# Chunked attention with its division deferred to the output stage, and with transposes ahead of the values matmuls

## The chip, the cores and the metric

The kernel runs on one core of a Trainium2 chip. The core has a matrix engine (TensorE, PE in the profile), VectorE (DVE), ScalarE (ACT), GpSimd (POOL) and SyncE (SP), which here does nothing but issue DMAs. Each engine works through its own instructions in program order; semaphores tie the engines together. The metric is the time of one execution on the device in microseconds, the median of several runs.

## What is computed

One layer of a streaming encoder: a combined input projection, two groups of attention heads, one output projection, a gated per-layer embedding and a LayerNorm. SEQ is 4096, D_MODEL 1024, all in float32. The change is in group A and in what reads its result.

```
def chunk_relbias_attention(q, k, v, rel_bias):      # 8 heads of 64, chunks of 64
    ...
    scores = jnp.einsum('bnqhd,bnkhd->bnhqk', qc, kb) * (d ** -0.5)   # own chunk and 8 before
    scores = scores + bias[None, None]
    scores = jnp.where(valid[None, :, None, None, :], scores, -jnp.inf)
    probs = jax.nn.softmax(scores, axis=-1)
    out = jnp.einsum('bnhqk,bnkhd->bnqhd', probs, vb)
...
ya = ya * jax.nn.silu(ag)
mix = jnp.concatenate([ya, yb], axis=-1) @ w_out     # yb: the sliding-window group
h = alpha * x + mix
h = h + jax.nn.sigmoid(h @ w_ple_gate) * (p @ w_ple_proj)
x = layer_norm(h, ln_g, ln_b)
```

## The kernel before

Every float32 factor of a product is split in a high and a low part of type fp32r (ScalarE copies the high part, VectorE subtracts it), so that two or three matmuls stand for one exact product. The program has four stages, written one behind the other for each engine.

**Projections** write q, k, v and the gates to DRAM.

**Stage A**, chunked attention. A unit is one head and one tile of 128 tokens (t, 0 to 31), 256 units in all; a turn of the hardware loop is two heads, 64 units. A tile attends to n = min(5, t + 1) tiles of 128 keys. Each engine has a function `a_step(it, i)` that says what it does in step i, each part with a lag: `a_unit(it, i, 4)` is the unit that was new four steps ago. For one unit: `a_scores` on TensorE writes scores into PSUM banks 0 and 1 (the only pair, `psum[:, 0:2]`); VectorE adds the bias and takes the maximum (L1115), then scales the maximum (L1130); ScalarE takes the exponential and its sum (L807); VectorE inverts the sum (L1125); ScalarE (L833), or for three tiles of eight VectorE (L1137), multiplies the probabilities by it; TensorE transposes them in five 128x128 pieces (`a_transpose`, L1404, lag 4) into banks 2 and 3 or 4 and 5; ScalarE and VectorE split them into pt_hi (L825) and pt_lo (L1103). For two units together `a_values` (lag 7) multiplies with v into bank 6 or 7. Its 128 output rows are two halves, by v's high and low part: ScalarE copies the lower 64 rows (L816), VectorE adds them to the upper ones (L1151). GpSimd multiplies four tiles' result with the gate (L683), and SyncE stores it to y_d and loads the next gate.

In a step TensorE issues first `a_values`, then `a_transpose`, then `a_scores` of the unit after the current.

**Stage B**, sliding-window attention: 64 units of four chunks; GpSimd applies the gate (L690), SyncE stores to y_d. At its end the weights of stage C are loaded and split in strips.

**Stage C**, the output, one tile of 128 tokens at a time. TensorE's loop: `mix(t + 1)`, 48 matmuls of 512 columns; `ple(t)`, 12; `gate(t)`, 48; `transpose_h(t + 1)`, eight transposes (L1542), which wait for the residual. VectorE's `c_step(t)`: y_lo of tile t + 2 (L1241), p_lo, the residual h of tile t + 1 (L1255), hT_lo, the LayerNorm of tile t (to L1297). ScalarE: y_hi of t + 2 (L898), p_hi, the sigmoid, hT_hi. GpSimd: the LayerNorm's scale and shift (L696, L698). SyncE, in this order:

```
def stage_c(t, i, more=True):
    sp.wait_ge(p_split, t + 1)
    load_tile(t + 2, i % 2)          # y_raw <- y_d, p_raw <- pT
    sp.wait_ge(h_done, t + 1)
    load_x(t + 1)                    # x_nat
    store_out(t, i % 3)              # waits for shifted, GpSimd's last pass on tile t
```

Since `store_out(t - 1)` stands ahead of `load_tile(t + 2)`, a tile of y is asked for only when the output of a tile three behind it is finished.

## Time and profile before

| | us |
|---|---|
| median of 3 runs | 2842.0 (2839.82 to 2842.2) |
| profiled execution, its span | 2843.8 |
| projections, to about | 1166 |
| stage A | 1166 to 1735 |
| stage B | 1735 to about 1990 |
| from B to C | about 1990 to 2022 |
| stage C | 2022 to 2843 |
| TensorE busy | 2692.4 (95%) |
| VectorE busy | 1398.1 (49%) |
| ScalarE busy | 1192.5 (42%) |
| GpSimd busy | 336.2 (12%) |

The shares are means over stages that differ much, so the stages are read one by one. TensorE's busy time is from modelled ends of pipelined matmuls that overlap; what a row of matmuls costs is read from the start of one to the start of the next. A name such as L1115 is a line of the kernel above. "Releaser" is what ended an engine's idle time.

### The profile page before, as it was taken

How to read it: one execution, taken by the hardware profiler on the slowest of the kernel's cores; microseconds unless marked ns; L12 is line 12 of the kernel's file. 1: busy time of each engine (PE TensorE's matmuls, PEld its weight loads, DVE VectorE, ACT ScalarE, POOL GpSimd, SP SyncE). 2: the span in 40 equal slices, each digit the busy share in tenths (PEclk: the TensorE clock that was granted, in tenths of full speed). 3: DMA queues.
4: the chain of work that ended last, by engine and by line, in shares of the span. 5: the costliest groups of instructions: out<-in, count | busy, mean ns of one | idle time of the engine just before them, and what ended most of it. 6: DMA issues, size and time to landing. Idle time of an engine off the chain costs nothing.

```text
span 2843.8 us, 40981 instructions
## 1 busy us (share of the span) xinstructions
PE 2692.4 (95%) x14544; PEld 2325.9 (82%) x14544; DVE 1398.1 (49%) x3367; ACT 1192.5 (42%) x2448; POOL 336.2 (12%) x227
## 2 busy tenths in 40 slices
PE   7999999999999999889989898987799999999997
PEld 5888888988888889878888888887688888888886
DVE  5211156232111461589989996778433334333343
ACT  3111122231111221589989997778322222222222
POOL 2000000000000000011111111334112221122211
PEclk9999999999999999999999997778899999999999
DMA  6431246453312463887767647785422211222111
GB/s 196 161 120 63 77 100 148 151 193 126 122 63 77 99 146 111 202 188 160 163 146 161 154 101 163 184 196 145 128 73 72 72 59 61 72 72 72 57 62 54
DMA packets 279246, 339.32 MB, mean 119 GB/s; under 512 B 81712, under 2 KB 201536, under 8 KB 274880
## 3 DMA queue, kind: packets, MB, share of 16 engines
q1 hardware_dynamic: 277648, 335.67, 43.8%
q0 software_dynamic: 1456, 1.86, 0.2%
q8 instruction: 76, 1.25, 0.2%
q14 instruction: 66, 0.54, 0.1%
HBM read 211.10 MB, written 127.41 MB: 119 GB/s over the span
## 4 chain that ended last, share of the span: by engine, by line
PE 71%; DVE 9%; issue 8%; ACT 6%; DMA 5%; POOL 1%; SPq 0%; ACTq 0%; DVEq 0%; POOLq 0%
PE psum L1338 68%; DVE pt_lo L1103 3%; ACT pt_hi L825 2%; ACT prob L807 2%; DMA y_d<-y_b 1%; DMA av<-v_d 1%; DMA x_raw<-in_xT 1%; PE psum L1542 1%; DVE y_a L1151 1%; ACT y_low L816 1%; DVE prob L1137 1%; PE psum L1489 1%; ACT prob L833 1%; POOL y_b L690 1%; ACT prob_b L855 0%
## 5 line engine op out<-in xcount | busy, mean ns | idle before, releaser
L1338 PE MATMUL psum<-x_hi,w_hi 128*128 128x512 f32 x1408 | 549.5, 390 | 20.1 <-DVE x_lo L1008 18.2
L1338 PE MATMUL psum<-x_hi,w_lo 128*128 128x512 f32 x1408 | 549.2, 390 | 0.0
L1338 PE MATMUL psum<-x_lo,w_hi 128*128 128x512 f32 x1408 | 549.1, 390 | 0.0
L1338 PEld LDWEIGHTS psum<-x_hi,w_hi 128*128 128x128 f32 x1408 | 265.3, 188 | 75.6 <-issue 18.2
L1338 PEld LDWEIGHTS psum<-x_lo,w_hi 128*128 128x128 f32 x1408 | 265.2, 188 | 55.3
L1338 PEld LDWEIGHTS psum<-x_hi,w_lo 128*128 128x128 f32 x1408 | 265.1, 188 | 55.1
L683 POOL TENSOR_TENSOR y_a<-y_a,g_a 64x512 f32<-64x512 f32 x64 | 81.4, 1272 | 1582.6 <-DVE y_a L1151 1582.6
L1338 PE MATMUL psum<-wo_hi,y_hi 128*128 128x512 f32 x512 | 204.8, 400 | 15.5 <-DVE y_lo L1241 10.0
L1404 PE MATMUL psum<-ident,prob 128*128 128x128 f32 x1200 | 182.4, 282 | 38.8 <-DVE pt_lo L1103 33.1
L1115 DVE CUSTOM_DVE_ANT_0 prob<-psum,bias 128x640 f32<-128x640 f32 (+4 forms) x256 | 198.8, 777 | 32.5 <-issue 30.3
L807 ACT ACTIVATE prob<-prob,small 128x640 f32<-128x640 f32 (+4 forms) x256 | 202.2, 790 | 27.2 <-DVE small L1130 22.4
L1241 DVE TENSOR_TENSOR y_lo<-y_raw,y_hi 128x1024 fp32r<-128x1024 f32 x32 | 39.2, 1225 | 347.4 <-ACT y_hi L898 347.4
L1103 DVE TENSOR_TENSOR pt_lo<-psum,pt_hi 128x640 fp32r<-128x640 f32 (+4 forms) x256 | 197.2, 770 | 15.3 <-ACT pt_hi L825 10.2
L1338 PE MATMUL psum<-wo_hi,y_lo 128*128 128x512 f32 x512 | 201.4, 393 | 0.0
L1338 PE MATMUL psum<-wo_lo,y_hi 128*128 128x512 f32 x512 | 201.0, 393 | 0.0
L1338 PE MATMUL psum<-wg_hi,hT_lo 128*128 128x512 f32 x512 | 199.4, 390 | 0.0
L1338 PE MATMUL psum<-wg_hi,hT_hi 128*128 128x512 f32 x512 | 199.2, 389 | 0.0
L1338 PE MATMUL psum<-wg_lo,hT_hi 128*128 128x512 f32 x512 | 199.2, 389 | 0.0
L1404 PEld LDWEIGHTS psum<-ident,prob 128*128 128x128 f32 x1200 | 129.9, 143 | 62.5 <-issue 55.0
L1048 DVE TENSOR_TENSOR stage_out<-psum,work 128x512 f32<-128x512 f32 x64 | 44.3, 692 | 273.2 <-ACT work L767 273.2
L1022 DVE TENSOR_TENSOR stage_out<-psum,stage_out 128x512 fp32r<-128x512 f32 x72 | 49.8, 691 | 251.6 <-ACT stage_out L742 226.6
L1338 PE MATMUL psum<-pt_hi,av 128*128 128x256 f32 x720 | 172.2, 275 | 0.8 <-DVE pt_lo L1103 0.8
(165 smaller groups left out, 5597.0 us busy)
## 6 DMA issues: line engine op xcount, KB each, us to landing
qk_d<-stage_out SPq DMA_DIRECT2D x80, 512.0 KB, 2.8
w_raw<-in_w_in SPq DMA_DIRECT2D x24, 1024.0 KB, 5.6
x_raw<-in_xT SPq DMA_DIRECT2D x32, 512.0 KB, 4.6
g_d<-stage_out SPq DMA_DIRECT2D x64, 256.0 KB, 2.0
bq_d<-stage_out SPq DMA_DIRECT2D x64, 256.0 KB, 4.1
v_d<-stage_out SPq DMA_DIRECT2D x32, 512.0 KB, 2.9
bq<-bq_d SPq DMA_DIRECT2D x64, 256.0 KB, 4.4
y_raw<-y_d SPq DMA_DIRECT2D x32, 512.0 KB, 4.8
```

The costliest lines, as they stand in the source:

```text
L683: pool.tensor_tensor(y_a[:, s, :], y_a[:, s, :], g_a[:, s, :], ALU.mult).then_inc(y_gated, 1)
L690: pool.tensor_tensor(yb, yb, g_b[:, s, :, :].rearrange("p h t -> p (h t)"), ALU.mult).then_inc(by_gated, 1)
L807: act.activation(prob[:, r, NBW - n * P:NBW], prob[:, r, NBW - n * P:NBW], ACT.Exp, bias=a_col(A_SHIFT, r), scale=SCALE, accum_out=a_col(A ...
L816: act.activation(y_low[:, pr % 2, :], psum[HEAD:P, 6 + pr % 2, 0:2 * P], ACT.Copy).then_inc(y_low_ready, 1)
L825: act.activation(pt_hi[:, (t // 2) % 2, e + BAND - n:e + BAND, e * P:e * P + P], src.rearrange("p (j q) -> p j q", q=P), ACT.Copy).then_in ...
L1022: dve.tensor_tensor(stage_out[:, slot, 1, :].bitcast(f32r), psum[:, bank, :], stage_out[:, slot, 0, :], ALU.subtract).then_inc(acc_free, 1)
L1048: dve.tensor_tensor(stage_out[:, r % 2, 0, :], psum[:, r % 8, :], work[:, r % 2, :], ALU.mult).then_inc(acc_free, 1)
L1103: dve.tensor_tensor(pt_lo[at], src.rearrange("p (j q) -> p j q", q=P), pt_hi[at].bitcast(f32), ALU.subtract).then_inc(probsT_split, 1)
L1115: dve.tensor_tensor_reduce(out=prob[:, r, NBW - n * P:NBW].rearrange("p (a b) -> p a b", a=2), in0=psum[:, 0:2, 0:n * P // 2], in1=bias[:, ...
L1241: dve.tensor_tensor(y_lo[:, :, :], y_raw[:, s, :, :], y_hi[:, :, :].bitcast(f32), ALU.subtract).then_inc(y_split, 1)
L1338: return pe.matmul(dst, lhs, rhs, start=start, stop=stop)
L1404: last = pe.transpose(psum[:, b, (j % 4) * P:(j % 4) * P + P], prob[:, t % RING, NBW - (n - j) * P:NBW - (n - j - 1) * P], ident[:, :])
```

## The change

The softmax's division is taken out of stage A. Scores and bias are combined so that their minimum serves directly as the exponential's bias, and the sums stay in `a_sum`; VectorE inverts the 32 sums of a head at once. The unnormalized result, still in its two halves, is copied by ScalarE (128x512, four tiles at once) and stored to `ya_d`. After the last head the inverses are transposed by TensorE, copied by ScalarE and stored to `ra_d`; stage B's first scores on TensorE wait for that copy. Sum of the halves, division and gate are now in stage C, on GpSimd, in `y_tile`. The split of the values matmuls into two parts and the order on TensorE are new, and the lags are shorter. The residual works in place in h (three slots), into which x is loaded.

```diff
 # SyncE, stage C
             def load_tile(t, s):
-                sp.dma_start(y_raw[:, s, :, :], y_d[:, bass.ds(t * P, P)].rearrange("(k p) t -> p k t", p=P)
+                cols = bass.ds(t * P, P)
+                sp.dma_start(y_two[:, s, :, :], ya_d[:, :, :, :, cols].rearrange("k c h d t -> (h d) (k c) t")
+                             ).then_inc(y_two_loaded[s], 16)
+                sp.dma_start(g_c[:, s, :, :], g_d[0:D_A, cols].rearrange("(k p) t -> p k t", p=P)
+                             ).then_inc(g_loaded[s], 16)
+                sp.wait_ge(g_scaled, t)
+                for hd in range(2):
+                    sp.dma_start(r_c[hd * HEAD:hd * HEAD + HEAD, :, :],
+                                 ra_d[:, hd, cols].unsqueeze(0).to_broadcast([HEAD, KT // 2, P])).then_inc(r_loaded, 16)
+                sp.dma_start(y_raw[:, s, KT // 2:KT, :], yb_d[:, cols].rearrange("(k p) t -> p k t", p=P)
                              ).then_inc(y_loaded[s], 16)
...
-            def stage_c(t, i, more=True):
-
+            def stage_c(t, i, stored, more=True):
+
+                slot = (i + 1) % 3
+                if stored is not None:
+                    sp.wait_ge(out_stored[slot], stored + 16)
+                load_x(t + 1, slot)
                 if more:
                     sp.wait_ge(p_split, t + 1)
                     load_tile(t + 2, i % 2)
-                sp.wait_ge(h_done, t + 1)
-                load_x(t + 1)
                 store_out(t, i % 3)
...
 # GpSimd
+            def y_tile(t, s, first=False):
+
+                two = y_two[:, s, :, :].rearrange("p (k c) t -> p k c t", c=2)
+                pool.wait_ge(y_two_loaded[s], 8 * (t - s) + 16)
+                if not first:
+                    pool.wait_ge(y_split, t - 1)
+                pool.tensor_tensor(y_raw[:, s, 0:KT // 2, :], two[:, :, 0, :], two[:, :, 1, :], ALU.add).then_inc(y_joined, 1)
+                pool.wait_ge(g_loaded[s], 8 * (t - s) + 16)
+                pool.wait_ge(r_loaded, 32 * t + 32)
+                pool.tensor_tensor(g_c[:, s, :, :], g_c[:, s, :, :], r_c[:, :, :], ALU.mult).then_inc(g_scaled, 1)
+                pool.wait_ge(y_joined, t + 1)
+                pool.wait_ge(g_scaled, t + 1)
+                pool.tensor_tensor(y_raw[:, s, 0:KT // 2, :], y_raw[:, s, 0:KT // 2, :], g_c[:, s, :, :], ALU.mult
+                                   ).then_inc(y_ready, 1)
...
+            with pool.Fori(0, 5) as it:
+                for i in range(6):
+                    y_tile(6 * it + i + 2, i % 2)
+                    scale_shift(6 * it + i, i % 3)
...
 # ScalarE
             def a_step(it, i):
-                unit = a_unit(it, i, 1)
+                unit = a_unit(it, i, 7)
+                if unit and unit[2] % 4 == 3:
...
+                    act.activation(y_a[:, slot, :], psum[:, 6 + quad % 2, :], ACT.Copy).then_inc(y_copied, 1)
+                unit = a_unit(it, i, 0)
...
             def y_tile_hi(t, s, first=False):
                 act.wait_ge(y_loaded[s], 8 * (t - s) + 16)
+                act.wait_ge(y_ready, t + 1)
...
 # TensorE
-            def a_values(u, pair, s, pr):
-                pe.wait_ge(probsT_split, u + 3)
-                pe.wait_ge(y_summed, pair + 1)
+            def a_values(u, it, quad, s, pr, part):
+
                 first_tile = 2 * pr - (BAND - 1)
...
+                order = [i for i in (1, 2, 0, 3, 4, 5) if first_tile + i >= 0]
+                half = (len(order) + 1) // 2
...
             def a_step(it, i):
-                unit = a_unit(it, i, 7)
-                if unit and unit[2] % 2 == 1:
-                    u, s, t = unit
-                    a_values(u, (A_TURN // 2) * it + (i - 7) // 2, s, t // 2)
-                unit = a_unit(it, i, 4)
+                unit = a_unit(it, i, 2)
                 if unit:
                     u, s, t = unit
-                    by_vector = t % 8 in VECTOR_NORMS
-                    a_transpose(u, t, normed[by_vector], norms(A_TURN - 1, by_vector) * it + norms(i - 4, by_vector))
-
+                    a_transpose(u, t)
+                for part, lag in ((1, 6), (0, 5)):
+                    unit = a_unit(it, i, lag)
+                    if unit and unit[2] % 2 == 1:
+                        u, s, t = unit
+                        a_values(u, it, (i - lag) // 4, s, t // 2, part)
```

On TensorE in the middle of stage A, before: a step with values, then one without, each instruction with its waits; `ident,prob` are transposes, `pt,av` values, `ak,aq` scores.

```order
L1338 MATMUL psum<-pt_hi,av 128x256 [waits y_summed,probsT_split]
L1338 MATMUL psum<-pt_lo,av 128x256
L1338 MATMUL psum<-pt_hi,av 128x256
L1338 MATMUL psum<-pt_lo,av 128x256
L1338 MATMUL psum<-pt_hi,av 128x256
L1338 MATMUL psum<-pt_lo,av 128x256
L1338 MATMUL psum<-pt_hi,av 128x128
L1338 MATMUL psum<-pt_lo,av 128x128
L1404 MATMUL psum<-ident,prob 128x128 [waits probsT_split,normed0]
L1404 MATMUL psum<-ident,prob 128x128 x4
L1338 MATMUL psum<-ak,aq_hi 128x320 [waits scores_used]
L1338 MATMUL psum<-ak,aq_hi 128x320
```

The same place after: in each step the transposes, then one half of a pair's values, then the scores.

```order
L1388 MATMUL psum<-ident,prob 128x128 [waits probsT_split,exp_done]
L1388 MATMUL psum<-ident,prob 128x128 x4
L1322 MATMUL psum<-pt_hi,av 128x256
L1322 MATMUL psum<-pt_lo,av 128x256
L1322 MATMUL psum<-pt_hi,av 128x256
L1322 MATMUL psum<-pt_lo,av 128x256
L1322 MATMUL psum<-pt_hi,av 128x128
L1322 MATMUL psum<-pt_lo,av 128x128
L1322 MATMUL psum<-ak,aq_hi 128x320 [waits scores_used]
L1322 MATMUL psum<-ak,aq_hi 128x320
L1322 MATMUL psum<-ak,aq_lo 128x320 x2
```

All values of a pair (eight rows here, twelve for a full band) stood in one step ahead of the transposes; now six stand in every step, behind them.

On SyncE in the loop of stage C, before; `out<-h` is the store of a tile, which waits for GpSimd's last pass.

```order
L614 DMA out<-h 128x1024 [waits shifted]
L559 ISA [waits p_split]
L559 DMA y_raw<-y_d 128x8x128
L561 DMA p_raw<-in_pT 128x2x128
L565 ISA [waits h_done]
L565 DMA x_nat<-in_x 128x1024
L614 DMA out<-h 128x1024 [waits shifted]
```

On SyncE in the same loop, after:

```order
L613 DMA out<-h 128x1024 [waits shifted]
L562 ISA [waits out_stored2]
L562 DMA h<-in_x 128x1024
L544 ISA [waits p_split]
L544 DMA y_two<-ya_d 128x8x128
L546 DMA g_c<-g_d 128x4x128
L550 DMA r_c<-ra_d 64x4x128 [waits g_scaled]
L550 ISA
L550 DMA r_c<-ra_d 64x4x128
L552 DMA y_raw<-yb_d 128x4x128
L558 DMA p_raw<-in_pT 128x2x128
L613 DMA out<-h 128x1024 [waits shifted]
```

x has moved ahead of the tile, and the tile's one DMA of y has become five; the store that waits for `shifted` is still ahead of all of them.

On GpSimd in the loop of stage C, before:

```order
L696 TENSOR_TENSOR h<-h,lng 128x1024 [waits normalized]
L698 TENSOR_TENSOR h<-h,lnb 128x1024 [waits scaled]
L695 REGISTER_ALU
L696 TENSOR_TENSOR h<-h,lng 128x1024 [waits normalized]
L698 TENSOR_TENSOR h<-h,lnb 128x1024 [waits scaled]
```

On GpSimd in the same loop, after:

```order
L702 TENSOR_TENSOR h<-h,lng 128x1024 [waits normalized]
L704 TENSOR_TENSOR h<-h,lnb 128x1024 [waits scaled]
L691 TENSOR_TENSOR y_raw<-y_two 128x512 [waits y_split,y_two_loaded1]
L693 ISA [waits g_loaded1]
L694 TENSOR_TENSOR g_c<-g_c,r_c 128x512 [waits r_loaded]
L695 REGISTER_ALU
L697 TENSOR_TENSOR y_raw<-y_raw,g_c 128x512 [waits g_scaled,y_joined]
L702 TENSOR_TENSOR h<-h,lng 128x1024 [waits normalized]
L704 TENSOR_TENSOR h<-h,lnb 128x1024 [waits scaled]
```

Each tile has three passes over 128x512 in front of the two over 128x1024 that it had.

## Rows read from the trace of the kernel before

**Rows 1.** The windows view, by stage: busy us per engine, granted clock, DMA share, GB/s.

```profile
66.00:1166.00 1100.00, 1100.00 (x5569) 942.41 (x5570) 328.95 (x529) 216.10 (x365) 1.25 (x2) 1.00 0.40 120
1166.00:1735.00 569.00, 504.04 (x3666) 452.13 (x3664) 509.49 (x1764) 523.65 (x1058) 81.43 (x64) 0.97 0.70 157
...
2022.00:2843.00 821.00, 804.96 (x3656) 667.65 (x3656) 303.15 (x542) 210.11 (x234) 148.18 (x62) 0.99 0.21 66
```

**Rows 2.** Groups by line, 1280 to 1720 us: busy us, mean ns | idle before.

```profile
L833 ACT ACTIVATE prob<-prob,small 128x640 f32<-128x640 f32 (+2 forms) x128 | 101.3, 791 | 0.0
...
L1151 DVE TENSOR_TENSOR y_a<-psum,y_low 64x256 f32<-64x256 f32 x103 | 42.2, 410 | 0.9
L1137 DVE TENSOR_SCALAR prob<-prob,small 128x640 f32<-128x640 f32 (+1 forms) x77 | 40.3, 524 | 0.0
L816 ACT ACTIVATE y_low<-psum 64x256 f32<-64x256 f32 x103 | 39.3, 381 | 4.0 <-PE psum L1338 1.5
```

**Rows 3.** The chain of what ended last, in stage A: start, us, what.

```profile
1490.36 0.71 DVE pt_lo L1103
...
1507.55 0.71 DVE pt_lo L1103
...
1515.95 2.04 PE psum L1338 x16
```

**Rows 4.** The timeline in stage A, TensorE and VectorE: start, us, instruction.

```profile
1505.07 0.73 PE L1404 MATMUL psum<-ident,prob 128*128 128x128 f32 x5
...
1505.55 0.54 PE L1338 MATMUL psum<-ak,aq_hi 128*128 128x320 f32 x2
...
1506.28 0.74 PE L1404 MATMUL psum<-ident,prob 128*128 128x128 f32 x5
...
1507.31 0.56 PE L1338 MATMUL psum<-ak,aq_hi 128*128 128x320 f32 x2 [0.30 <-DVE small L1115]
...
1508.30 0.82 DVE L1115 CUSTOM_DVE_ANT_0 prob<-psum,bias 128x640 f32<-128x640 f32 x1
```

**Rows 5.** The chain over the whole span, end of the first head.

```profile
1205.35 33.59 DMA av<-v_d
```

**Rows 6.** The timeline of VectorE: first tile of head 1, last tile of head 7.

```profile
1240.22 0.29 DVE L1115 CUSTOM_DVE_ANT_0 prob<-psum,bias 128x128 f32<-128x128 f32 x1
...
1720.08 0.82 DVE L1115 CUSTOM_DVE_ANT_0 prob<-psum,bias 128x640 f32<-128x640 f32 x1
```

**Rows 7.** The chain in stage C: two groups of transposes of h.

```profile
2480.62 0.87 PE psum L1542 x8
...
2506.02 0.87 PE psum L1542 x8
```

**Rows 8.** The timeline in stage C, GpSimd, SyncE, ScalarE and VectorE.

```profile
2492.60 2.39 POOL L698 TENSOR_TENSOR h<-h,lnb 128x1024 f32<-128x1024 f32 x1
2495.01 0.37 SPq L614 DMA_DIRECT2D out<-h  x1
2495.92 0.38 SPq L559 DMA_DIRECT2D y_raw<-y_d  x1
2500.34 1.06 ACT L898 ACTIVATE y_hi<-y_raw 128x1024 fp32r<-128x1024 f32 x1 [6.56 <-DMA y_raw<-y_d]
2502.91 1.22 DVE L1255 SCALAR_TENSOR_TENSOR h<-x_nat,psum 128x1024 f32<-128x1024 f32 x1
```

**Rows 9.** Costliest groups on the page: GpSimd's gating in stage A.

```profile
L683 POOL TENSOR_TENSOR y_a<-y_a,g_a 64x512 f32<-64x512 f32 x64 | 81.4, 1272 | 1582.6 <-DVE y_a L1151 1582.6
```

**Rows 10.** The timeline from B to C, TensorE and GpSimd [idle before <-releaser].

```profile
1977.70 1.08 PE L1489 MATMUL psum<-ident,prob_b 128*128 128x128 f32 x4 [3.41 <-DVE ptb_lo L1174]
...
1999.83 0.79 PE L1338 MATMUL psum<-wo_hi,y_hi 128*128 128x512 f32 x1 [10.04 <-DVE y_lo L1241]
...
2002.28 2.03 POOL L690 TENSOR_TENSOR y_b<-y_b,g_b 64x512 f32<-64x512 f32 x1 [3.76 <-DMA g_b<-g_d]
...
2021.79 0.79 PE L1338 MATMUL psum<-wo_hi,y_hi 128*128 128x512 f32 x1 [5.49 <-DVE wp_lo L1228]
```

More of the change, by code:

```diff
@@ L78 @@
 ALPHA32 = float(np.float32(ALPHA))
-def norms(v, by_vector):
-    n = (v + 1) // 8 * len(VECTOR_NORMS) + sum(t < (v + 1) % 8 for t in VECTOR_NORMS)
-    return n if by_vector else v + 1 - n
 def b_unit(u):
@@ L201, in build @@
         lng, lnb = (sb(n, [P, D_MODEL]) for n in ("lng", "lnb"))
-        h = sb("h", [P, 3, D_MODEL])
+        h1, h2 = (sb(n, [P, D_MODEL]) for n in ("h1", "h2"))
+        sb("strip_end", [P, D_MODEL])
+        h0 = sb("h0", [P, D_MODEL])
+        g_c = sb("g_c", [P, 2, KT // 2, P])
+        r_c = sb("r_c", [P, KT // 2, P])
+        y_hi, y_lo = (sb(n, [P, KT, P], f32r) for n in ("y_hi", "y_lo"))
+        h = (h0, h1, h2)
         stage.close()
@@ L522, in _ @@
             sp.sem_inc(p_over, 1)
-            for q in range(QSLOTS):
-                load_gate(0, q)
             for part in range(JB, PARTS):
@@ L622, in _ @@
             sp.sem_inc(b_over, 1)
+            for t in range(2):
+                load_p(t, t)
             sp.wait_ge(cw_split, len(strips))
@@ L928, in _ @@
             p_tile_hi(1, 1, True)
+            act.wait_ge(cw_split, len(strips))
             hT_tile_hi(0)
```

266 lines of the change are left out of this document (125 added, 141 removed).

## The prediction

> **What bounds the kernel now.** I first cut the span by stage [rows 1]. The projections (66 to 1166 us) keep TensorE busy for every microsecond and are not touched. Chunked attention (stage A, 1166 to 1735) has TensorE busy 504 of 569 us, VectorE 509 and ScalarE 524: three engines near their limit. Sliding-window attention (stage B, 1735 to 1990) does the same work before and after. The output stage (stage C, from 2022) is TensorE again, 805 of 821 us. A reader should see two kinds of stage: in A a cut on VectorE and ScalarE can pay, in C only something that makes TensorE wait can change the time.
>
> **Stage A, what goes.** Between 1280 and 1720 us [rows 2] ScalarE spends 101.3 us in the normalizing copy L833 and 39.3 in the 64-row copy L816, and VectorE 40.3 in L1137 and 42.2 in the add L1151. All four go, with two one-column operations per tile on VectorE. ScalarE gets one 128x512 copy per four tiles; at the price of the 128x640 passes (about 0.8 us) that is 0.2 us a tile. Both engines fall from about 90% (524 and 509 of 569 us) to some 65 to 75%, so neither sets the pace.
>
> **Stage A, what is late next.** TensorE has the same matmuls as before. Its cost for two tiles comes from start to start [rows 3, 4]: one score group with twelve values matmuls 2.04 us, the other score group 0.73 (1505.55 to 1506.28), two groups of transposes 0.48 each (1505.07 to 1505.55). The sum is 3.73, or 1.87 us a tile. A second ring is as long: scores write a single pair of banks, so they start at 1507.31, the VectorE pass on them at 1508.30, and it ends at 1509.12, after which the next scores may start: 1.81 us. The new order fits both: in the 0.9 us in which VectorE holds the banks, TensorE has the transposes (0.48) and half of a pair's values ((2.04 - 0.73) / 2 = 0.66). So TensorE is the bound, at 1.87 or above. What stands behind it is the wait of the transposes for pt_lo, which follows the bias pass on VectorE and now ends at about the time the scores end; I add 0.1 and take 1.97. The period now is 17.19 us for eight tiles, 2.15 each (in [rows 3] 1490.36 and 1507.55 are the same step of the pattern of eight).
>
> Seven heads run from 1240.22 to 1720.08 [rows 6]. Each has 28 full tiles, which gain 28 x 0.18 = 5.0 us, and four short ones, for which I take 1 us together: 7 x 6 = 42 us. The first head ends in a wait for the load of av, issued at 1205.35 and landed 33.59 us later behind everything else in the queue [rows 5]. Faster compute doesn't shorten that; four gate loads of 128 KB fewer do, by about 2 us. **Stage A: -44 us.** Bounds: -60 if TensorE runs at 1.87 with no wait and the short tiles gain 2 us a head, -20 if the waits between the three engines bring the period to 2.08. The reciprocals are turned into rows once, by two transposes and one copy, in front of B: 1 to 2 us, taken as covered by the shorter drain (lag 6 for 7). B itself does the same work.
>
> **Stage C, the wait that the change adds.** Here the division and the sum of the halves now lie. Follow one tile [rows 7, 8]. The transposes of h start at 2480.62, and the next ones at 2506.02: 25.4 us, all of it TensorE. Beside it runs a chain which nearly fills that time. GpSimd's second pass on the output ends at 2494.99 (2492.60 + 2.39), SyncE stores it at 2495.01 and only then, in program order, issues y_raw for two tiles on, at 2495.92. It lands and ScalarE splits it from 2500.34. VectorE subtracts, and after that, again in program order, does the residual, 2502.91 to 2504.13. The transposes need that residual, and it is there 1.9 us before they are due. So TensorE bounds this stage with less than 2 us to spare.
>
> The change puts three things into that chain. First, SyncE now issues x in front of the tile, then y_two, g_c, twice r_c, y_raw and p. By the end of r_c the queue has moved, beyond what it moves now by the end of y_raw, x (0.5 MB) and g_c and r_c (0.25 MB each): 1.05 MB with y_two in y_raw's place. The rate of the full queue follows from stage C: 66 GB/s at a share of 0.21 [rows 1] make 0.31 MB per us. That is 3.3 us: r_c lands at about 2503.7, and y_two at about 2502.3. Second, GpSimd does three passes of 512 columns, for which the row is its pass over 64x512, 1.27 us [rows 9]. The join runs under the r_c load; the scaling of the gate and the product follow it: 2503.7 + 2.6 = 2506.3. Third, ScalarE and VectorE go on as before, y_hi to the end of the residual 3.8 us (2500.34 to 2504.13): 2510.1. The transposes are due at 2506.02 and start at 2510.1. **+4.1 us a tile**, and since the next tile's chain starts with these transposes, the delay is not absorbed but comes again with each.
>
> Bounds. Below: y_two lands no earlier than y_raw does now, plus 0.5 us for the x issue ahead of it (2500.8), and GpSimd's three passes are in order, 3.8 us: 2504.6, residual 2508.4, so +2.4. Above: seven DMAs' own overhead and slow small packets, another 2 us: +6.1.
>
> The array's clock comes on top. After an idle stretch of 3.41 us in stage B [rows 10] it stands at the lower of its two levels: four transposes take 1.08 us there, where stage C's eight take 0.87 [rows 7]. Transposes after each stall would take twice as long, 0.87 us more, and they are on the chain; the matmuls after them are not, since TensorE then has time to spare. I take +0.8, nearly every tile.
>
> The Trainium skill ("TensorE: Matmul & The Clock Gate", in "Why this matters for your kernels") says that idle gaps between bursts of matmuls send the array back to its lower clock; by its rule the 0.87 comes in all tiles, 2 us more in the total than I take. [rows 10] agree. On the load the skill ("DMA: Bandwidth & Descriptors", in "Anatomy of one DMA") has a variable part of bytes by 436 GB/s; as an estimate by it the 1.05 MB would take 2.4 us for my 3.3, and the total would be some 27 us lower. Stage C's row shows 0.31 MB per us, and the measurement decides.
>
> The loop loads tiles 2 to 31; tile 2's load waits for no store, and the last h isn't behind a tile's load. That leaves 29 groups of transposes: 29 x (4.1 + 0.8) = **+142 us**. Bounds 29 x 2.4 = 70 and 29 x 6.9 = 200.
>
> **From B to C.** The first tile's load now needs GpSimd, which is in order behind B's last gating, 2002.28 + 2.03 = 2004.3 [rows 10]. Three passes, y_hi and y_lo (about 2.2) put the first product at 2010.3, where it starts at 1999.83 now. Three more DMAs sit ahead of B's last gate loads, some 2 us. It ends in the same way: the array waits until 2021.79 for the last strips, whose splits stand behind y_hi of tile 1 and so behind that product. **+12 us**, bounds +5 (the strips, not the product, are late) and +18.
>
> **The sum** against the profiled execution: 2843.8 - 44 + 142 + 12 = 2953.8 us. The median of the runs is 1.8 below the profiled span: 2952 us, 3.9% slower.
>
> **Rivals.**
> 1. *Stage C absorbs it; the result is faster.* If y_hi could start by about 2502.2, 1.9 us later than now, TensorE would never wait, and the whole would be 2842 - 44 + 9, about 2807. For it: engines other than TensorE are idle most of stage C (GpSimd 148 of 821 us by [rows 1]), and the y load was always waited for, not computed. Against it: even the bound from below puts y_hi at 2504.6, 2.4 us past that point, and two GpSimd passes (2.5 us) alone exceed the slack. It needs GpSimd's passes at less than half of their row and x's transfer hidden. 8%.
> 2. *Stage C stalls by the lower bound with no clock loss, and A gains all:* 2842 - 60 + 70 + 5 = 2857, still 0.5% slower: one end of the main case, within its chance.
> 3. *Stage A gains nothing.* The new order might trade the saturated engines for the ring of scores and bias pass: at 2.08 us a tile or more, A gives 20 or less, and the sum is 2976 or more, about 2980. For it: that ring measures 1.81 us before any jitter, and TensorE 1.87. Against it: the two overlap fully on paper. 12%.
> 4. *The change does not do what it says in A:* if the first half of the values waits for pt_lo of its own pair, the order brings nothing over values first. Its pair is three steps behind the scores on VectorE and five on TensorE, so it doesn't wait. Only the division's cut would count; 2970. 3%.
>
> **How the numbers follow.** Main case, 75%: 2952, with its own range of 2857 to 3010. Rival 3 and 4, 15%: 2970 to 2980. Rival 1, 8%: 2807. Between them, C stalling by 1 to 2 us only, 2%: about 2840. The range is 2865 to 3010: the main case and rivals 3 and 4, short of the corner in which all of the main case's bounds fall low together. A run of this kernel repeats within 0.1% and a comparison can tell about 0.2%. Faster by over 0.2%: 0.09; within: 0.02; slower: 0.89.
>
> **What the changed profile would show.** In stage A bias passes 1.9 to 2.0 us apart, ScalarE and VectorE near 70%, heads of some 61 to 64 us, and waits of the transposes on pt_lo. In stage C transposes of h 29.5 to 30.5 us apart, each after an idle stretch of 3 to 4 us that VectorE's residual ends, ScalarE's y_hi released by GpSimd, and a granted clock visibly under 1. I am wrong if the transposes of h stay 25.4 us apart, or if y_hi starts less than 2 us later in its tile than now.

## The result, and the profile after

The changed kernel takes **3048.6 us** (median of 4 runs, 3045.5 to 3054.7) against 2842.1 (2839.8 to 2845.4): a ratio of 1.0724, 95% interval 1.0708 to 1.0740. It is 7.2% slower. The forecast was 2952, 3.9% slower, with a range up to 3010: the sign was right, the size was not.

The windows view of the changed kernel, by stage (columns: window, its length, busy us of PE, PEld, DVE, ACT, POOL with instruction counts, granted TensorE clock, DMA share, GB/s):

```profile
66.00:1166.00 1100.00, 1098.20 (x5573) 940.94 (x5571) 329.28 (x536) 217.31 (x369) 0.00 (x0) 1.00 0.40 120
1164.00:1675.00 511.00, 484.86 (x3695) 454.84 (x3696) 385.79 (x1050) 401.39 (x858) 0.00 (x0) 0.97 0.76 177
1676.00:1956.00 280.00, 214.52 (x1372) 207.12 (x1370) 196.43 (x448) 197.80 (x719) 94.19 (x67) 0.73 0.71 173
1976.00:3052.00 1076.00, 879.28 (x3656) 721.85 (x3656) 303.50 (x543) 213.76 (x235) 263.16 (x152) 0.90 0.28 72
```

The last row answers to stage C's in [rows 1]: the same 3656 matmuls and transposes, in 1076 us for 821, at a clock of 0.90 for 0.99. TensorE was 98% busy there and is 82% busy now. The second row answers to stage A's: VectorE and ScalarE are at 75 and 79%, at or a little above the forecast's 65 to 75%, and the stage is shorter.

Five points of the program, read from the two timelines, cut the 209.0 us between the two profiled executions (2843.8 and 3052.8) into pieces:

| stretch | before | after | difference | forecast |
|---|---|---|---|---|
| start to first bias pass | 1167.4 | 1164.4 | -3.0 | 0 |
| first to last bias pass (A) | 552.6 | 490.3 | -62.4 | |
| last bias pass to B's first scores | 15.3 | 11.7 | -3.6 | A in all: -44 |
| B's first scores to C's first product | 264.5 | 289.7 | +25.2 | |
| C's first product to its loop | 22.0 | 20.0 | -2.0 | B to C: +12 |
| C's loop to the end | 822.0 | 1076.8 | +254.7 | +142 |

The first row isn't the change's doing: in the profiles of kernels below that are the same up to this point the first bias pass starts at 1163.6 to 1167.3.

**Stage C, one period.** The timeline of the changed kernel from a tile's last pass on GpSimd to the next transposes of h; it answers to [rows 7, 8]. Numbers in brackets are the idle time before an instruction and what ended it. The last line is from the kernel before, at the same point of its loop.

```profile
2491.85 2.39 POOL L704 TENSOR_TENSOR h<-h,lnb 128x1024 f32<-128x1024 f32 x1
...
2494.27 0.37 SPq L613 DMA_DIRECT2D out<-h  x1
2494.83 0.36 SPq L562 DMA_DIRECT2D h<-in_x  x1
2495.39 0.56 SPq L544 DMA_DIRECT2D y_two<-ya_d  x1
2496.04 0.87 SPq L546 DMA_DIRECT2D g_c<-g_d  x1
2497.01 1.44 SPq L550 DMA_DIRECT2D r_c<-ra_d  x2
...
2501.24 1.29 POOL L691 TENSOR_TENSOR y_raw<-y_two 128x512 f32<-128x512 f32 x1 [7.00 <-DMA y_two<-ya_d]
2506.08 1.28 POOL L694 TENSOR_TENSOR g_c<-g_c,r_c 128x512 f32<-128x512 f32 x1 [3.55 <-DMA r_c<-ra_d]
2507.51 1.26 POOL L697 TENSOR_TENSOR y_raw<-y_raw,g_c 128x512 f32<-128x512 f32 x1
...
2511.37 1.22 DVE L1239 SCALAR_TENSOR_TENSOR h<-h,psum 128x1024 f32<-128x1024 f32 x1
...
2512.64 1.97 PE L1538 MATMUL psum<-ident,h 128*128 128x128 f32 x8 [5.43 <-DVE h L1239]
...
2480.45 1.03 PE L1542 MATMUL psum<-ident,h 128*128 128x128 f32 x8
```

The chain runs as the prediction describes it: store, loads, join, scaling, product, split, residual, transposes; then through the LayerNorm to the next store at 2528.10. Two links are longer than forecast. GpSimd waits for r_c until 2506.08, 11.8 us behind the store, where I had 8.7. And all the transposes behind a stall run at the lower clock: 1.97 us, after an idle stretch of 5.43, for 1.03 to 1.04 in the same view of the kernel before. (The 0.87 of [rows 7] is from the chain, which counts only from the end of the matmul in front.) From store to store the loop takes 34.15 us on average over 28 tiles; before it took 25.41.

**Where r_c is late.** The DMA view of stage C (2020 to 3000 us), median us from issue to landing:

```profile
y_two<-ya_d SPq DMA_DIRECT2D x28, 512.0 KB, 5.6
r_c<-ra_d SPq DMA_DIRECT2D x58, 128.0 KB, 7.6
y_raw<-yb_d SPq DMA_DIRECT2D x29, 256.0 KB, 8.6
g_c<-g_d SPq DMA_DIRECT2D x28, 256.0 KB, 6.1
```

128 KB of r_c, issued 1.6 us behind 512 KB of y_two, land later after their issue than y_two after its own. Each of its two loads reads four rows of 128 reciprocals and writes them to 64 partitions: 256 packets of 512 bytes, all from the same four places.

What the DMA engines do meanwhile, the windows view shows for the period above (columns: window, its length, busy us of GpSimd, granted clock, DMA share, GB/s):

```profile
2495.00:2502.00 7.00, 0.76 (x1) 1.00 0.99 282
2502.00:2505.00 3.00, 0.54 (x1) 1.00 0.31 72
```

From 7.7 us behind the store the rate falls to a quarter, and the engines are busy a third of the time; r_c is there at 2506. In the mean of 26 tiles the rate from 7 to 10 us behind the store is 57 GB/s. The queue isn't full there; it moves slowly.

**From B to C.** GpSimd at the end of B:

```profile
1933.01 1.26 POOL L682 TENSOR_TENSOR y_b<-y_b,g_b 64x512 f32<-64x512 f32 x1 [1.85 <-DMA g_b<-g_d]
1945.35 1.26 POOL L682 TENSOR_TENSOR y_b<-y_b,g_b 64x512 f32<-64x512 f32 x1 [11.09 <-DMA g_b<-g_d]
1948.44 1.25 POOL L682 TENSOR_TENSOR y_b<-y_b,g_b 64x512 f32<-64x512 f32 x1 [1.82 <-DMA g_b<-g_d]
1949.65 1.25 POOL L691 TENSOR_TENSOR y_raw<-y_two 128x512 f32<-128x512 f32 x1
```

The last gate load but one lands 11 us late. On SyncE the five loads of tile 0 are issued just ahead of it (1931.91 to 1935.13), the slow r_c among them. And the join of tile 0 stands behind all 64 gate passes.

### The profile page after: what moved, and what is told of

It is laid out like the page before. It is cut to its first block, busy times and chain, and to the rows that moved or that the text cites. A ratio compares the mean times of both kernels' runs of the same rounds, so it can differ in the third digit from the quotient of the medians.

```text
span 3052.8 us, 39860 instructions
## 1 busy us (share of the span) xinstructions
PE 2738.8 (90%) x14546; PEld 2375.1 (78%) x14546; DVE 1269.0 (42%) x2638; ACT 1068.3 (35%) x2225; POOL 376.1 (12%) x257
## 4 chain that ended last, share of the span: by engine, by line
PE 44%; issue 16%; DVE 15%; DMA 10%; POOL 9%; SPq 3%; ACT 3%; DVEq 0%; POOLq 0%; ACTq 0%
PE psum L1322 41%; DMA y_two<-ya_d 5%; DVE pt_lo L1132 5%; POOL h L704 2%; POOL h L702 2%; DMA g_b<-g_d 2%; PE psum L1538 2%; POOL g_c L694 1%; POOL y_raw L697 1%; DVE sg L1254 1%; DVE h L1257 1%; DMA yb_d<-y_b 1%; DMA av<-v_d 1%; DVE h L1239 1%; ACT y_hi L907 1%
## 5 line engine op out<-in xcount | busy, mean ns | idle before, releaser
L682 POOL TENSOR_TENSOR y_b<-y_b,g_b 64x512 f32<-64x512 f32 x64 | 90.5, 1415 | 1794.6 <-DVE y_b L1197 1655.2
L1322 PE MATMUL psum<-wo_hi,y_hi 128*128 128x512 f32 x512 | 224.8, 439 | 31.6 <-DVE y_lo L1227 26.8
L1538 PE MATMUL psum<-ident,h 128*128 128x128 f32 x256 | 60.2, 412 | 182.1 <-DVE h L1239 182.1
L1322 PE MATMUL psum<-wo_lo,y_hi 128*128 128x512 f32 x512 | 218.1, 426 | 0.0
L1322 PE MATMUL psum<-wo_hi,y_lo 128*128 128x512 f32 x512 | 216.1, 422 | 0.0
L1538 PEld LDWEIGHTS psum<-ident,h 128*128 128x128 f32 x256 | 48.2, 215 | 195.0 <-DVE h L1239 194.8
L1322 PE MATMUL psum<-pt_hi,av 128*128 128x256 f32 x720 | 191.1, 294 | 0.0
L1322 PE MATMUL psum<-pt_lo,av 128*128 128x256 f32 x720 | 169.4, 283 | 0.0
```

Of the source, the lines that this page charges most:

```text
L682: pool.tensor_tensor(yb, yb, g_b[:, s, :, :].rearrange("p h t -> p (h t)"), ALU.mult).then_inc(by_gated, 1)
L1322: return pe.matmul(dst, lhs, rhs, start=start, stop=stop)
L1538: last = pe.transpose(psum[:, 2 + k // 4, (k % 4) * P:(k % 4) * P + P], h[slot][:, k * P:k * P + P], ident[:, :])
```

## Experiments

All are built on the changed kernel. "Period" is the mean time from store to store in C's loop, over the 28 periods from the second store on; the clock is the granted clock over the same stretch.

| run | us | period | C loop's clock |
|---|---|---|---|
| before | 2842.1 | 25.41 | 1.00 |
| changed kernel | 3048.6 | 34.15 | 0.90 |
| e1_ahead | 2799.8 | 25.41 | 1.00 |
| e2_ahead_values_first | 2786.0 | 25.37 | 1.00 |
| e3_no_r | 2932.7 | 30.02 | 0.96 |
| e4_r_distinct | 2983.5 | 31.92 | 0.93 |
| e5_x_behind | 3079.5 | 35.04 | 0.89 |
| e6_fill | 3051.3 | 34.00 | 0.95 |
| e7_ahead_late0 | 2789.5 | 25.37 | 1.00 |
| e8_ahead_late0_values_first | 2783.8 | 25.37 | 1.00 |
| e9_ahead_late0_turn_between | 2783.0 | 25.41 | 1.00 |
| e10_r_before_x | 3149.2 | 37.60 | 0.86 |

e3 to e6 and e10 are one run each.

### Is it where the loads stand?

e1_ahead loads a tile one store earlier:

```
     def stage_c(t, i, stored, more=True):
...
         if more:
-            sp.wait_ge(p_split, t + 1)
-            load_tile(t + 2, i % 2)
+            sp.wait_ge(p_split, t + 2)
+            load_tile(t + 3, (i + 1) % 2)
         store_out(t, i % 3)
```

(with tile 2 loaded ahead of the loop, and the last six of its tiles written out behind it).

> The changed kernel, with one thing moved: SyncE asks for the tile of three steps on, before it waits to store the present one, instead of asking for the tile of two steps on behind that wait. Same DMAs, same GpSimd passes. Theory 1 (the loss in stage C is a chain through the store's wait, the loads, GpSimd, the residual and back): the transposes of h come 25.4 us apart again (now 33.8), stage C gives back 29 x 8.4 = 244 us, and the kernel takes about 3049 - 244 = 2805 us. Rival (contention: stage C's 1500 more small packets or GpSimd's passes slow the other engines, wherever they stand): the spacing stays above 28 us and the kernel above 2880.

Measured: 2799.8 us, ratio 0.9845 (0.9829 to 0.9862) to the kernel before. The period is back at 25.41, all of it TensorE. The loads are nearly as slow as in the changed kernel (r_c lands after 7.2 us, median, for 7.6), but they are asked for about 24 us ahead of their use. From its timeline, in one period:

```profile
2499.49 0.37 SPq L613 DMA_DIRECT2D out<-h  x1
...
2502.10 1.29 POOL L701 TENSOR_TENSOR y_raw<-y_raw,g_c 128x512 f32<-128x512 f32 x1
2503.42 1.06 ACT L911 ACTIVATE y_hi<-y_raw 128x1024 fp32r<-128x1024 f32 x1 [5.17 <-POOL y_raw L701]
2505.99 1.21 DVE L1243 SCALAR_TENSOR_TENSOR h<-h,psum 128x1024 f32<-128x1024 f32 x1
...
2510.33 1.04 PE L1542 MATMUL psum<-ident,h 128*128 128x128 f32 x8
```

The product no longer follows the store, and the residual ends 3.1 us before the transposes are due. So the stall of stage C needs the place of the loads behind the store: with it mended, neither their slowness nor GpSimd's three passes cost anything.

### What in the loads is slow?

e3_no_r leaves out the loads of r_c in the loop, so from tile 2 on (t is a plain number for tiles 0 and 1 only; the gates of the later tiles are scaled with a stale r_c, and GpSimd waits for the first two only); its other work is as in the changed kernel.

```
-                sp.wait_ge(g_scaled, t)
-                for hd in range(2):
-                    sp.dma_start(r_c[hd * HEAD:hd * HEAD + HEAD, :, :],
+                if isinstance(t, int):
+                  sp.wait_ge(g_scaled, t)
+                  for hd in range(2):
+                    sp.dma_start(r_c[hd * HEAD:hd * HEAD + HEAD, :, :],
...
```

> The changed kernel, without the loads of the inverse sums r_c for tiles 2 to 31 (their result is then divided by another tile's sums); GpSimd's three passes stay. The scaling no longer waits for r_c (landed 11.8 us after the store's issue). If the r_c loads are what my sum had too small, the three passes run back to back behind y_two: y_hi at about 11 us after the store's issue for 14.5, transposes of h 30.2 to 30.6 us apart for 33.8, total about 2945. If they only share a queue whose last bytes come at the same time anyway (y_raw's second half bounds y_hi), the spacing stays at 32 or more, total above 3000.

Measured: 2932.7 us, 116 less than the changed kernel, and 4.13 us less between stores: 30.02. That is about the period which I had forecast *with* these loads (25.4 + 4.9 = 30.3).

e4_r_distinct keeps two loads of 128 KB in r_c's place, of the same packets, but each partition reads a row of its own (gate rows, so the scaling uses wrong numbers).

```
 ...
-   ra_d[:, hd, cols].unsqueeze(0).to_broadcast([HEAD, KT // 2, P])
+   g_d[hd * 256:hd * 256 + 256, cols].rearrange("(k p) t -> p k t", p=HEAD)
 ...
```

> The changed kernel, with r_c filled from 256 different rows of the gates (two DMAs of the same shape, packets and bytes) instead of eight rows read 64 times each; the result is then scaled by something else. The trace of the changed kernel has the first r_c 2.5 us and the second 1.45 us behind the DMA ahead of each, for 256 packets that should take 0.7. If reading the same rows again and again is slow, r_c lands 2 us earlier and the transposes of h come about 31.8 us apart, total about 2990. If 64 partitions as destination, or the number of DMAs, is the reason, nothing changes: 33.8, 3048.

Measured: 2983.5 us, a period of 31.92. So of the 4.13 us that r_c's loads cost per tile (34.15 - 30.02), 1.90 are two more loads of any kind, and 2.23 come from reading the same four places 64 times. In e4 these loads land after 6.0 us (median), where r_c's take 7.6. A part of both figures is the clock: the transposes take 1.97 us a tile in the changed kernel, 1.80 in e4 and 1.47 in e3, since shorter stalls leave some groups at the higher level. (What I expected counts 0.7 us for 256 packets; by the prediction's 0.31 MB per us it is 0.4.) The slow stretch is gone from the windows view of e4, at the same distance from its store (2587.76):

```profile
2595.00:2597.00 2.00, 1.18 (x1) 1.00 1.22 232
```

Over 26 tiles the mean rate from 7 to 10 us behind the store is 186 GB/s here, for 57 in the changed kernel.

### Is it the bytes in front of r_c?

Two runs move x, 512 KB, relative to the slow loads. e5_x_behind issues x last:

```
-                load_x(t + 1, slot)
                 if more:
                     sp.wait_ge(p_split, t + 1)
                     load_tile(t + 2, i % 2)
+                load_x(t + 1, slot)
```

> The changed kernel, with the load of x issued behind the tile's loads instead of ahead of them. My sum had 1.7 us for x ahead of r_c (0.5 MB at 0.31 MB per us); by packets (128 of 4 KB) it is 0.9 us and 0.55 us of issue on SyncE. Expected: r_c lands 0.9 to 1.7 us earlier, transposes of h 32.1 to 32.9 us apart for 33.8, total 3000 to 3025. If the loads are limited by something else than the bytes ahead of them (the issue of each DMA, the landing of r_c itself), 33.5 or more.

Measured: 3079.5, 31 us *slower* than the changed kernel. The gain that I expected fell; of the other case the period holds (35.04, where it had 33.5 or more), though it had nothing in it that makes the kernel slower. (The 0.9 us for x has no row behind it: 0.5 MB in 0.9 us are 0.58 MB per us, and no stretch read here shows more than 0.4.) y_two landed 4.7 us after its issue for 5.6, as it should; but in the period read, r_c's product starts at 2518.57, 12.6 us behind the store at 2505.99, for 11.8 in the changed kernel. The windows view of that period:

```profile
2512.00:2516.00 4.00, 0.89 (x1) 1.00 0.28 43
```

The slow stretch begins 6.0 us behind the store, for 7.7: x's bytes in front did cost about the 1.7 us that the prediction counts for them. But from there r_c takes 6.6 us more, for 4.1 in the changed kernel, and that eats the gain and more. Why this stretch is longer I can't say.

e10_r_before_x does the opposite: p_raw and r_c are issued first, then x, y_two, g_c and y_raw.

> The changed kernel, with the two loads of r_c issued behind the store and ahead of x, y_two and g_c (p_raw's small load in front of them). Theory (the re-read rows are slow by themselves): r_c still lands 7 us or more after its issue, so its product starts about 2 us a tile sooner and no more: about 2990 us (2970 to 3010). Rival (r_c is late because 1.5 MB stands in front of it): it lands 2 to 4 us after its issue, the bound passes to y_two and y_raw, and the time is that of the run without r_c's loads or a little more, 2930 to 2955.

Measured: 3149.2, 100 us slower than the changed kernel, and outside both forecasts. Its DMA view:

```profile
h<-in_x SPq DMA_DIRECT2D x26, 512.0 KB, 9.6
y_two<-ya_d SPq DMA_DIRECT2D x26, 512.0 KB, 10.8
r_c<-ra_d SPq DMA_DIRECT2D x52, 128.0 KB, 7.5
g_c<-g_d SPq DMA_DIRECT2D x26, 256.0 KB, 11.1
```

The half of the theory on r_c held: with only the store and 128 KB in front it still needs 7.5 us, as in the changed kernel (7.6). The slow stretch shows most clearly here, where little stands in front of it:

```profile
2503.00:2509.00 6.00, 0.00 (x0) 1.00 0.26 49
```

From the beginning of the slow stretch to r_c's arrival it is more than 6 us here and in e5, the two kernels that have x behind r_c, and 4.1 us in the changed kernel; what this hangs on is open. What I had left out is that everything issued behind r_c waits for it: y_two takes 10.8 us for 5.6, and GpSimd's join starts at 2514.52, 14.3 us behind the store at 2500.27. The slow loads stand in one queue with the others, and whoever comes behind them pays. The Trainium skill ("DMA: Bandwidth & Descriptors", in "Queues, rings and completion order") says that each DMA engine consumes its descriptors in ring order; the trace agrees, 10.8 us against 5.6.

### What is the clock worth?

e6_fill issues 16 extra matmuls, whose result is overwritten, ahead of the transposes of h, to fill the idle stretch.

```
                     gate(t)
+                    for _ in range(16):
+                        mm(psum[:, 2, :], wo_hi[:, 0, 0:P], wg_hi[:, 0, 0:512], True, True)
                     transpose_h(t + 1, (i + 1) % 3)
```

> The changed kernel, with 16 matmuls of 512 columns added in front of each group of transposes of h in stage C, into a bank that is free then; what they compute is overwritten. They fill 3.6 us of a stall of 5.4. If the array's lower clock behind the stall costs time on the chain, the granted clock in stage C goes from 0.90 to near 1, the eight transposes take about 0.9 us for 1.98, and the spacing falls by 1.1 us: total about 32 us lower, 3016. If the clock costs nothing on the chain, the total stays at 3048, or rises if 16 matmuls reach past the residual.

Measured: 3051.3, no gain. In its profile 12 of 29 groups of transposes took 1.0 to 1.1 us and 16 still 1.97; together they take 46.0 us where the same 29 take 56.2 in the changed kernel, some 10 us less, but the mean period fell only by 0.15, 4 us over the loop, and a single run does not tell that from nothing. The filler takes 3.8 us, and about 3.5 us of idle time remained in front of the transposes, so the stall that brings the lower level was only cut short. What the clock costs is better read off the rows: 0.93 us more per group than in the kernel before (1.97 for 1.04). What getting it back would bring by itself stays open. That the level goes with the idle stretch, one more row shows: in e3, where TensorE waits less, some groups keep the higher clock:

```profile
2600.49 1.10 PE L1539 MATMUL psum<-ident,h 128*128 128x128 f32 x8 [2.60 <-DVE h L1240]
```

### The order of transposes and values

e2 is e1 with one more edit, in stage A's step on TensorE: the half pair of values ahead of the transposes.

```
+                for part, lag in ((1, 6), (0, 5)):
+                    ...
+                        a_values(u, it, (i - lag) // 4, s, t // 2, part)
                 unit = a_unit(it, i, 2)
                 if unit:
                     u, s, t = unit
                     a_transpose(u, t)
-                for part, lag in ((1, 6), (0, 5)):
-                    ...
```

> As e1_ahead, but in stage A each step issues its half of the values matmuls ahead of the transposes: the order half of the change undone, the deferred division kept. If the order matters, pt_hi and pt_lo of a tile come 0.66 us later behind the transposes, the transposes no longer fill the time right behind the scores, and the bias passes are 1.95 to 2.05 us apart for 1.9: 12 to 30 us more than e1_ahead. If only the division mattered (the engines are at 70% and have slack), no difference: within 5 us of e1_ahead.

Measured: 2786.0, ratio 0.9799 (0.9783 to 0.9815): 14 us *faster* than e1, whose interval it doesn't touch. Both forecasts fell. First to last bias pass, e1 takes 489.6 us and e2 478.1. The changed kernel in the middle of a head, TensorE and VectorE:

```profile
1380.51 0.82 DVE L1116 CUSTOM_DVE_ANT_0 prob<-psum,bias 128x640 f32<-128x640 f32 x1 [0.39 <-issue]
1381.26 0.82 DVE L1132 TENSOR_TENSOR pt_lo<-psum,pt_hi 128x640 fp32r<-128x640 f32 x1
...
1382.22 0.74 PE L1388 MATMUL psum<-ident,prob 128*128 128x128 f32 x5
1382.72 0.36 PE L1322 MATMUL psum<-pt_hi,av 128*128 128x256 f32 x1
...
1383.45 0.50 PE L1322 MATMUL psum<-ak,aq_hi 128*128 128x320 f32 x2
...
1384.29 0.82 DVE L1116 CUSTOM_DVE_ANT_0 prob<-psum,bias 128x640 f32<-128x640 f32 x1 [0.38 <-issue]
```

pt_lo ends at 2.08 (of 1380), and 0.14 later the transposes start, which stand right behind the scores; the values take until 3.45, the scores until 4.25, and the next but one bias pass starts at 4.29. That is a loop of 3.78 us for two tiles, 1.89 each (1.88 in the mean of all full tiles). Most of it is TensorE's own row: from the transposes to the values 0.46 to 0.50 us, the values 0.73, the scores 0.35 and 0.30, which is 1.84 without a wait. With the values first (e2), in the same place:

```profile
1380.12 0.28 PE L1326 MATMUL psum<-pt_hi,av 128*128 128x256 f32 x1
...
1380.33 0.82 DVE L1120 CUSTOM_DVE_ANT_0 prob<-psum,bias 128x640 f32<-128x640 f32 x1 [0.25 <-issue]
...
1380.77 0.73 PE L1392 MATMUL psum<-ident,prob 128*128 128x128 f32 x5
...
1381.26 0.54 PE L1326 MATMUL psum<-ak,aq_hi 128*128 128x320 f32 x2
1381.64 0.46 PE L1326 MATMUL psum<-ak,aq_lo 128*128 128x320 f32 x2
1381.93 0.28 PE L1326 MATMUL psum<-pt_hi,av 128*128 128x256 f32 x1
...
1382.14 0.82 DVE L1120 CUSTOM_DVE_ANT_0 prob<-psum,bias 128x640 f32<-128x640 f32 x1 [0.25 <-issue]
```

The pt_lo pass before these transposes (1379.26, 0.82 us) ended at 0.08, 0.7 us ahead of them. Nothing on TensorE waits any more: values 0.65 us (from 1380.12), transposes 0.49, scores 0.67, and at 1381.93 the next values, 1.81 us on. The windows view of four tiles, e2's and then the changed kernel's (busy us of PE, PEld, DVE, ACT, POOL), says the same by the weight loads:

```profile
1380.12:1387.38 7.26, 7.26 (x63) 7.26 (x62) 6.25 (x16) 6.44 (x14) 0.00 (x0) 1.00 1.02 235
1380.31:1387.87 7.56, 7.56 (x63) 7.16 (x62) 6.26 (x16) 6.42 (x16) 0.00 (x0) 1.00 1.03 241
```

PEld is busy all of the time in e2 and 7.16 of 7.56 us in the changed kernel. So in e2, in most steps, TensorE itself sets the period, at 1.81. The ring of scores and bias pass stands close behind it: the pass ends at 1.15 and the scores start at 1.26, while scores that do wait for a pass (as at 1366.80 us) start 0.06 to 0.07 us behind its end; the ring alone would make 1.76 to 1.78. That 1.81 is also the figure which the prediction had for this ring is chance.

e9 tests the loop. It has e7's edits (below), and the transposes stand behind two of the six values matmuls. e8 has the values all ahead.

> As the kernel before it in this call, but in stage A a step's transposes stand behind the first two of its six values matmuls: neither ahead of all nor behind all. Theory (a loop): in the changed kernel a bias pass, the exponential, the transposes, the values matmuls and the scores follow one another and come back to the bias pass every 3.79 us for two tiles, because the transposes stand right behind the scores and wait for the exponential (0.08 us too much per tile). Two matmuls in front of the transposes (0.24 us) then end that wait: stage A as with the values first, 2776 (2770 to 2783). Rival (switching): TensorE loses the time each time it goes from one kind of matmul to another; there is one more such change here, so no faster than with the transposes first, 2790 or more.

> All three moves together: tile t+3 loaded ahead of the store of tile t, tile 0's loads behind the last gate load, and in stage A the values matmuls ahead of the transposes. If the three gains lie in different stages they add up: the first two gave 2789.5 us and the third took 13.8 us off, so 2776 (2770 to 2782). If putting tile 0's loads late and ending stage A sooner spend the same slack of the gate chain, this stays at 2784 to 2789.

Measured: e9 2783.0 (ratio 0.9797, 0.9776 to 0.9817), e8 2783.8 (0.9782, 0.9757 to 0.9808; the interval reaches into both of its forecasts), e7 without either 2789.5 (0.9812, 0.9789 to 0.9835). The intervals overlap, so the totals don't separate them. The profiles do, in stage A: from first to last bias pass e7 takes 489.4 us, e9 481.6, e8 475.2, and e9's passes are 1.82 apart where one reads 1.81 in e8. Two matmuls ahead of the transposes end the wait in the full tiles, as the loop says: the transposes now start 0.28 us behind pt_lo, for 0.14 where they wait for it. That TensorE would lose the 0.07 us a tile by changes between kinds of matmul is out, since e9 has one change more. A small price of them there is: the six values take 0.73 us behind transposes and 0.65 behind scores, of which the starts of transposes and scores give back 0.06, and e9's passes are 1.82 apart for e8's 1.81. Why e9's stage A is still 6.4 us longer than e8's, these rows don't explain in full. One link was named wrongly in what I expected: it is not the exponential. At a head's start the widths tell the tiles apart:

```profile
1354.07 0.39 ACT L828 ACTIVATE prob<-prob,small 128x128 f32<-128x128 f32 x1
...
1357.56 0.82 DVE L1132 TENSOR_TENSOR pt_lo<-psum,pt_hi 128x640 fp32r<-128x640 f32 x1
...
1356.87 0.28 PE L1388 MATMUL psum<-ident,prob 128*128 128x128 f32 x1
...
1358.53 0.41 PE L1388 MATMUL psum<-ident,prob 128*128 128x128 f32 x2
```

Tile 0's exponential is over at 1354.46, 2.4 us before its one transpose (the third row). Tile 1's two transposes (the last row) follow pt_lo's end at 1358.38 by 0.15: what they wait for is pt_lo of the tile two before, whose banks they overwrite. The prediction had this wait in view.

### From B to C

e7 is e1 with tile 0's loads moved behind B's last gate load:

```
                     if u + 1 < B_ALL:
                         load_bgate(u + 1)
+                    if u == B_ALL - 2:
+                        load_tile(0, 0)
```

(and taken from their old place, ahead of the last two gate loads).

> As e1_ahead, with the five loads of stage C's first tile issued behind stage B's last gate load instead of ahead of the last two. Between B's first scores and the first product of C the changed kernel has 290 us where the kernel before has 264. If the first tile's loads hold up B's last gates (GpSimd idles 11 us ahead of the second last), the stretch falls by 6 to 10 us and so does the total: about 2797. If the time was lost elsewhere in B, or y_hi of the first tile is simply later, no change or a few us more.

Measured: 2789.5, ratio 0.9812 (0.9789 to 0.9835): 10 us less than e1, whose interval it just touches. The 64 gate passes of B on GpSimd are a chain of loads, passes and stores; their start times, relative to the first, in us:

| pass | before | after | e1 | e2 | e7 | e8 | e9 |
|---|---|---|---|---|---|---|---|
| second | 6.2 | 12.7 | 6.9 | 13.0 | 13.5 | 6.8 | 6.5 |
| 57th | 208.7 | 223.1 | 215.0 | 217.5 | 214.7 | 217.0 | 209.2 |
| last | 237.8 | 258.8 | 251.3 | 253.5 | 246.7 | 246.6 | 240.3 |

The first pass itself starts 29 us behind B's first scores in before, e1, e8 and e9 and 23 in the others, and those are the kernels in which the second comes at 6 to 7: the second pass stands at 35 to 37 us in all of them.

The last seven passes take 29.1 us before, 35.7 to 36.3 where tile 0's loads stand ahead of the gate loads, and 29.6 to 32.0 where they stand behind. In e4, which has the loads ahead but reads distinct rows, they take 31.5: here too it is r_c's rows that cost most of it. The middle of the chain differs by as much between kernels with the same code there: the 57th pass comes 246.4 us behind B's first scores in the changed kernel and 237.5 to 246.0 in the others, 237.9 before. One profile of each can't say that the change adds anything there, and 6 of e7's 9 us between B's first scores and C's first product are of this kind.

After the last pass the changed kernel needs 7.6 us to C's first product, where before the product started 2.5 us *ahead* of the last pass, since ScalarE then split y_raw and needed no GpSimd. That 10.1 us is the join in GpSimd's queue, as forecast (10.5).

In the profiles the gains don't all add up: e8's stage A is 14.2 us shorter than e7's, and its first product in C starts only 3.8 us sooner (1940.80 for 1944.57). Of the rest 8 us are in the chain of gate loads, whose 57th pass comes 246.0 us behind B's first scores in e8 and 238.0 in e7; whether the shorter stage A causes that or the spread named above, isn't shown.

## Why the prediction was right and wrong

**Stage C, +142 forecast, +254.7 measured: the failed step, by size.** The mechanism stood: the added loads and two GpSimd passes behind the store, the residual pushed past the transposes, the loss coming again with every tile. The two GpSimd passes and ScalarE's start took 2.72 us (2506.08 to 2508.80) for 2.6, y_hi to the residual's end 3.79 for 3.8. Wrong was the term "That is 3.3 us: r_c lands at about 2503.7". It turned bytes into time by the full queue's rate, 8.7 us behind the store; r_c came after 11.8, and that is 3.1 of the 3.5 us that the period shown (33.8) is over my 30.3. In the mean of 26 tiles it is 12.1, so 3.4 of the 3.8 us by which the mean period (34.15) is over. The rate of 0.31 MB per us was read from stage C's stores and loads, which all go to and come from distinct rows; while r_c's rows are read it is 0.07. I did have "slow small packets" as a bound, of 2 us, but no row stood behind that figure. That it is r_c's loads, e3 shows: without them the period is 30.02; that it is their rows, e4: with distinct ones it is 31.92. My upper bound of 6.9 a tile was passed by the 8.7 measured.

**The clock, +0.8 forecast.** All 29 groups ran at the lower clock and took 0.93 us more, 1.97 for 1.04, so mechanism and size held, and "nearly every tile" was every tile. It is 4 of the 113 us. One reading was off without harm: the 0.87 of [rows 7] is a piece of the chain and the 1.08 of [rows 10] a row of the timeline, and the two views count a group differently. The Trainium skill ("TensorE: Matmul & The Clock Gate", in "Why this matters for your kernels") says that idle gaps between bursts of matmuls send the array back to its lower clock, and by that the prediction had the loss in all tiles; the trace agrees, 29 of 29 groups at 1.97 us.

**Stage A, -44 forecast, -66 measured.** Bias passes are 1.88 us apart in the mean; I had taken 1.97 and given 1.87 as TensorE's floor. Seven heads are 58.2 us shorter for 42, the first head 4.2 for 2, and the end of the stage 3.6. That TensorE is the bound was right. Its floor was too high: e2 runs the same matmuls at 1.81 and the changed order has a row of 1.84. The wait on pt_lo was there as described, but the 0.1 us added for it was too much: from the scores' second pair to the transposes it is 0.37 us in one step (1381.85 to 1382.22) and 0.30, which is no wait, in the next (1383.79 to 1384.09). My bound of -60 was worked out wrongly as well: 28 x 0.28 + 2 us a head is 9.8, so 69 for seven heads, and with the first head's 2 it is -71.

**The order.** "The new order fits both" was right against the kernel before, and blind to the alternative: rival 4 asked only whether the order acts, not whether it hurts. It does act, and it costs 11.5 us of stage A (e1 against e2), some 14 in the total. What stage A gained comes from the division, the split values and the lags, not from transposes first; no run takes those three apart.

**B to C, +12 forecast, +23.2 measured.** The join behind GpSimd's last pass was there with 10.1 us. The loads ahead of the last gate loads cost 7, not 2, again because r_c is among them (e4: 31.5 us for the last seven passes, the changed kernel 35.7). The other 6 are the gate chain up to its 57th pass, 8.5 us later behind B's first scores, less 2.0 at the end. That part was no term of mine, and its cause stays open; by the spread named above it need not be the change's.

**Rivals.** Stage C absorbed nothing; stage A gained more than forecast, so rival 3 is out. The range ended at 3010 because its upper end took C's +200 with A's -44: with the measured A it would have ended at 2988. Of the 113 us by which C was over, r_c's late landing is about 99 (29 x 3.4) and the clock 4. That the total missed by 97 us and not by more is luck: stage A missed by 22 us the other way.

## What to carry to other kernels

A load's time is not its bytes by the queue's rate: count its packets and ask whether they read the same addresses, and remember that everything issued behind it in the queue waits too. When a stage is bound by one engine with 2 us to spare, new work may go beside it, but not behind the store of the tile before: loading one store earlier turned +7.2% into -1.6%. And when an order of instructions is chosen for one engine, write down for both orders what its own row costs and what the loop through the other engines costs; here transposes first came to a row of 1.84 us and a wait on pt_lo, 1.88 in all, and values first to a row of 1.81 without one.

With the loads a store earlier and the values ahead of the transposes, the kernel with the deferred division is 2.0% faster than the one before (e2: 0.9799, 0.9783 to 0.9815); with tile 0's loads behind the gate loads as well, it is 2.2% (e8: 0.9782, 0.9757 to 0.9808), which doesn't differ measurably.

## What was not expected of the hardware

- Two loads of 128 KB, each of which reads four rows 64 times, land 7.5 to 7.6 us after issue, behind 1.25 MB of other loads or behind 128 KB; of distinct rows 6.0; the 512 KB load ahead of them 5.6. The difference is 2.2 us per tile in the loop.
- While they are read the DMA engines are mostly idle: share 0.31 and 72 GB/s in the changed kernel, 0.26 and 49 in e10, where distinct rows (e4) have 1.22 and 232.
- They hold up what is behind them: a 512 KB load lands after 10.8 us behind them, 5.6 in front of them.
- Moving 512 KB from in front of them to behind them made them start 1.7 us sooner behind the store and land 0.8 us later. The longer stretch is not explained.
